# Identity matmuls into an unused bank at idle steps of the mLSTM and GLA mixers

## What is computed

```python
ha = head_rms(mlstm)  * sigmoid(ao)     # A: mLSTM, chunkwise matrix memory with a running maximum
hb = head_rms(gla)    * silu(bg)        # B: gated linear attention, chunkwise
hc = window_fn(rope(cq), rope(ck), cv)  # C: dilated sliding windows over a cache of 2048 rows
hd = sb_fn(dq, dk, dv, b_sb)            # D: stick-breaking attention over paged keys and values
mixed = concatenate([ha, hb, hc, hd]) @ w_out
```

## Time and profile before

| | us |
|---|---|
| median of 3 runs | 2581.53 (2580.14 to 2583.04) |
| the profiled execution, its own time | 2581.21 |
| its span, first to last instruction | 2579.6 |
| TensorE busy in the span | 2360.4 |
| mixers, first layer | 525 to 914 |
| mixers, second layer | 1795 to 2181 |

### The profile page before, as it was taken

How to read it: one execution, slowest core, us unless ns; L and a number is a source line. 1 busy time by engine, 2 the same in 40 slices (tenths; PEclk the granted TensorE clock), 3 DMA queues, 4 the chain that set the end, 5 groups by cost and what they waited for, 6 DMA issues and landing times. The chain is left out here.

```text
span 2579.6 us, 44886 instructions
## 1 busy us (share of the span) xinstructions
PE 2360.4 (92%) x17622; PEld 2094.7 (81%) x17622; DVE 1217.7 (47%) x2088; ACT 933.5 (36%) x1645; POOL 141.3 (5%) x193
## 2 busy tenths in 40 slices
PE   7999999979787889999999999999897877999997
PEld 7999998756545589999999999977564555999997
DVE  6343362253665556332453425522447555653325
ACT  5222342223324455223352334222333255542233
POOL 0000010011221000000000000000112110000000
PEclk8999999989897899999999999999898888999998
DMA  5232343154664343323333333421556535423233
GB/s 136 66 98 82 84 124 121 33 173 147 198 166 138 118 147 83 98 69 94 99 84 82 81 86 111 130 83 55 185 169 185 177 99 168 115 66 98 65 104 97
DMA packets 384957, 290.97 MB, mean 113 GB/s; under 512 B 51808, under 2 KB 368392, under 8 KB 384272
## 3 DMA queue, kind: packets, MB, share of 16 engines
q1 hardware_dynamic: 368128, 234.08, 32.2%
q0 software_dynamic: 16128, 54.54, 6.9%
q10 hardware_dynamic: 528, 0.02, 0.0%
HBM read 274.99 MB, written 13.58 MB: 112 GB/s over the span
## 5 line engine op out<-in xcount | busy, mean ns | idle before, releaser
L218 PE MATMUL ps<-h_hi,w_hi 128*128 128x288 f32 x2400 | 717.8, 299 | 25.0 <-PEq L174 17.9
L219 PE MATMUL ps<-h_lo,w_hi 128*128 128x288 f32 x2400 | 710.2, 296 | 0.0
L220 PE MATMUL ps<-h_hi,w_lo 128*128 128x288 f32 x2400 | 710.1, 296 | 0.0
L242 DVE TENSOR_TENSOR w_lo<-w_raw,w_hi 128x2048 fp32r<-128x2048 f32 x145 | 332.4, 2292 | 340.0 <-ACT w_hi L236 339.9
L218 PEld LDWEIGHTS ps<-h_hi,w_hi 128*128 128x128 f32 x2400 | 452.2, 188 | 31.3 <-issue 25.8
L219 PEld LDWEIGHTS ps<-h_lo,w_hi 128*128 128x128 f32 x2400 | 452.3, 188 | 0.9
L220 PEld LDWEIGHTS ps<-h_hi,w_lo 128*128 128x128 f32 x2400 | 452.2, 188 | 0.0
L236 ACT ACTIVATE w_hi<-w_raw 128x2048 fp32r<-128x2048 f32 x145 | 276.8, 1909 | 163.4 <-PE ps L220 159.1
L218 PE MATMUL ps<-f_a_hi,w_hi 128*128 128x288 f32 x1024 | 302.8, 296 | 0.0
L220 PE MATMUL ps<-f_a_hi,w_lo 128*128 128x288 f32 x1024 | 301.6, 295 | 0.0
L219 PE MATMUL ps<-f_a_lo,w_hi 128*128 128x288 f32 x1024 | 301.5, 294 | 0.0
(11 more groups left out here) (347 smaller groups left out, 3204.3 us busy)
## 6 DMA issues: line engine op xcount, KB each, us to landing
w_raw<-in_w_ffn_in SPq DMA_DIRECT2D x132, 512.0 KB, 5.2
w_raw<-in_w_ffn_out SPq DMA_DIRECT2D x80, 512.0 KB, 4.9
sa_vn<-in_cache_sb_v SPq DMA_DIRECT2D x256, 128.0 KB
w_raw<-in_w_in SPq DMA_DIRECT2D x52, 512.0 KB, 4.5
sa_vn<-in_cache_win_v SPq DMA_DIRECT2D x96, 128.0 KB
w_raw<-in_w_out SPq DMA_DIRECT2D x24, 512.0 KB, 6.5
sa_kn_early<-in_cache_win_k POOLq DMA_DIRECT2D x72, 128.0 KB
sa_vn<-in_cache_win_v SPq DMA_DIRECT2D x16, 512.0 KB
```

The lines of the kernel that those rows point to most:

```text
L218: pe.matmul(out, stat_hi, mov_hi, start=start, stop=False, skip_group_check=True)
L219: pe.matmul(out, stat_hi, mov_lo, start=False, stop=False, skip_group_check=True)
L220: return pe.matmul(out, stat_lo, mov_hi, start=False, stop=stop, skip_group_check=True)
L242: dve.tensor_tensor(E["w_lo"][:, slot], E["w_raw"][:, slot], E["w_hi"][:, slot].bitcast(F32), ALU.subtract).then_inc(S["w_lo"], 1)
```

## The change

A new function issues n matmuls of the identity with itself, each of which overwrites the first 128 columns of a bank that nobody reads at that point. It is called in mLSTM with 6 matmuls ahead of each of the ticks 1, 2 and 3 (steps 2 to 4) and at the head of step 5, with 4 at the end of step 35 and with 6 in each of steps 36, 37 and 38; in GLA with 6 in each of steps 4 and 5. That makes 58 in a layer. The wait for the copied queries moves from step 6 of GLA to the head of step 4.

```diff
--- before.py
+++ after.py
@@ -1337,6 +1337,12 @@
                        "n_turned n_copied")
 
 
+def keep_busy(pe, E, bank, n):
+
+    for _ in range(n):
+        pe.matmul(E["ps"][:, bank, 0:P], E["ident"][:], E["ident"][:], start=True, stop=True, skip_group_check=True)
+
+
 def mlstm(nc, E, M, l, I, O, C, side):
 
 
@@ -1602,9 +1608,10 @@
 
     def tensor_program(pe):
         yield
-        yield
-        yield
-        yield
+        for _ in range(3):
+            keep_busy(pe, E, SC, 6)
+            yield
+        keep_busy(pe, E, SC, 6)
         pe.wait_ge(S["exps_done"], 3)
         n = TILES * H
         for k, row in enumerate((wrow, ws, em)):
@@ -1692,8 +1699,11 @@
         pe.wait_ge(S["s_state_added"], 2 * H)
         pe.transpose(ps[:H, NB, 0:HD], pc[:, :, HD], E["ident"][:HD, :HD])
         pe.transpose(ps[:4 * H, NB, P:2 * P], c0[:, :, :, HD].rearrange("p q h -> p (q h)"), E["ident"][:]).then_inc(S["n_turned"], 1)
-        yield
-        yield from head_tensor(pe, E, S, hA, 2)
+        keep_busy(pe, E, SC, 4)
+        yield
+        for step in head_tensor(pe, E, S, hA, 2):
+            keep_busy(pe, E, SC, 6)
+            yield
 
     return dict(sync=sync_program, tensor=tensor_program, scalar=scalar_program, vector=vector_program)
 
@@ -1916,10 +1926,11 @@
         mm.then_inc(S["pre_done"], 1)
         yield
         yield
-        yield
-        yield
+        pe.wait_ge(M["mx"]["ro_q_out"], TILES)
+        for _ in range(2):
+            keep_busy(pe, E, ATT, 6)
+            yield
         pe.wait_ge(S["factors_ready"], 4)
-        pe.wait_ge(M["mx"]["ro_q_out"], TILES)
         pe.wait_ge(M["mx"]["ro_k_out"], TILES)
 
         def inside(t):
```

## The result

| | us |
|---|---|
| before, median of 5 runs beside it | 2581.42 (2579.19 to 2583.04) |
| after, median of 5 runs | 2593.22 (2590.86 to 2594.15) |
| ratio after to before | 1.0046, 95% interval 1.0031 to 1.0061 |
| the profiled execution of after, its own time and span | 2592.61 and 2591.0 |

The account below looks back on a forecast made before the run. In the mixers TensorE waits, mostly for copies by ScalarE and VectorE. First layer -1.0 + 0.9 - 0.9 = -1.0 us, second +0.3 + 1.1 - 0.9 = +0.5, together -0.5: 2581.0 us, range of all 2575 to 2590.

Parts of the forecast that it names:

- the last one of the sum: Later steps of the stage: ticks 1 to 2 us late find keys and values loaded ahead; counted as nothing.
- GLA: Steps 4 and 5 up to tick 32: 12 matmuls hidden, clock stays up, scores come sooner; -0.9 us in each layer.
- The heads: mLSTM's heads, 22 matmuls: +0.9 us in the first layer, +1.1 us in the second.
- the 2.05 us for step 38's six: mLSTM's heads, behind L1322 towards L1915: nothing hides these six, clock rises in their midst; 2.05 us, first layer.
- The pause of 6.1 us: mLSTM's heads, TensorE's wait for ScalarE's copy: cut to 3 us by steps 36 and 37, half clock still behind it.
- The start: Start of the mixers, 24 matmuls: -1.0 us in the first layer, +0.3 us in the second.
- The sign that I named for it: Start of the mixers, trace after: L1489 about 1 us earlier against the start of the stage, first layer.
- The gain of 1.0 us: L1622 to L1489, first layer: with the clock up these take 1.0 us less and VectorE goes on sooner.
- The first six: Start of the mixers, ahead of tick 1's transposes: 1.3 us, passed through to VectorE's chain.
- the fourth six: Start of the mixers, behind tick 4's transposes, which should find full clock: cost 1.3 us.
- The slower rival: Added matmuls paid at half clock ahead of L1622 and L1915, GLA giving nothing back: +11.2 us, 2593; chance 0.20.
- The faster rival: Clock stays up past the heads too: -4.9 us, about 2576, or 2573 with shorter later half-clock stretches; chance 0.20.

Follow-up runs that it names:

- gla_only: The kernel before with only GLA's 12 matmuls a layer (steps 4 and 5) and the moved wait: 2584.98 us, ratio 1.0026.
- start_only: The kernel before with only the 24 matmuls a layer at the start of mLSTM: 2581.27 us, ratio 1.0005.
- stair_ten: The kernel before with ten identity matmuls a layer in the prompt's attention (851 us), at full clock: 2590.93 us, ratio 1.0068.
- fill_alone: The kernel before with eight identity matmuls a layer in the 2.31 us pause of the prompt's attention, leaving bank 7's sum alone: 2579.61 us, ratio 0.9995.
- stair_four: The kernel before with four identity matmuls a layer in the prompt's attention (851 us), at full clock: 2581.12 us against 2573.44, ratio 1.0031.
- one_column: The whole change, all 116 matmuls and the moved wait, but each matmul multiplies one column in place of 128: 2598.85 us, ratio 1.0080.

## Why the prediction was wrong

**The step that failed** is the last one of the sum: "a tick that comes 1 to 2 us later has its keys and values loaded several units ahead; I count nothing for them". That was argued for transfers, and all that stands behind tick 32 was put at nothing. But how long the clock is at half in those later steps changed. The distance from tick 32 to the mark went from some 166.9 us (three of the four readings of before; 168.4 in the other) to 173.0 us in both layers: 6.1 us twice. Against the second trace of before it is 6.3 us in the first layer, in three places: 2.1 us over GLA's last updates (with step 38's six), 1.9 us some 100 us behind tick 32 and 2.3 us at the end of the prompt's attention (both with GLA's matmuls alone too).

The 12.2 us of this do not add up with the rest to the 11.8 us measured. Against the second trace of before the changed kernel's trace loses 12.3 us behind tick 32 and 5.7 us ahead of it, but that execution of before was the fastest of its ten (2575.4 us). Against the first trace it is 10.7 us behind and 1.9 us ahead, with 1.2 us gained elsewhere. So two thirds or more of the loss are behind tick 32; a finer split is not known.

**What stood ahead of it was right for GLA and too low for the rest.** GLA: forecast -0.9 us in each layer up to tick 32, measured -0.9 and -1.0 from L1925 to there in after, -0.7 and -0.8 in gla_only; tick 32 took 1.06 us for 1.09 forecast, and the clock stayed up. The heads: forecast +0.9 and +1.1, measured +2.0 and +2.3 from L1693 to L1915. The term that was mis-sized is the 2.05 us for step 38's six: they took 2.93 us, at half clock in both layers, in each trace that has them with 128 columns. The pause of 6.1 us was cut to 3.15 as forecast. The start: forecast -1.0 and +0.3; start_only's ratio of 1.0005 does not tell that from nothing. The sign that I named for it failed: L1489 was to come 1.0 us earlier in the first layer, counted from L1451, and came at 32.31 us against 30.36 and 28.66 in the two traces of before. The gain of 1.0 us was read from one trace in which L1622 happened to be at half clock. The first six took 2.93 us in the first layer of after and 1.60 us in its second layer and in start_only, where I had 1.3, and the fourth six 2.39 in the first layer.

**The rivals.** The slower rival had the right sign and nearly the right time (2593, itself past the 2590 at which I ended the range). Its mechanism was payment ahead of L1622 and L1915 at half clock, with GLA's 12 matmuls free. One part of it is borne out: step 38's six ran at half clock to their end and cost some 2 us a layer where they stand, for its 3.1. The rest is not: start_only costs nothing measurable, and GLA's part costs 6.7 us. So the near hit in the number is luck. The faster rival's condition, full clock from L1322 on, did not occur: after was at half from 685.3 to 695.3. It said that shorter half-clock stretches later in the stage might give 3 us more; they do move, but the other way.

**Shown and argued.** Shown: most of the loss sits in steps behind the added matmuls, at stretches of half clock; an unrelated delay of 1.0 us gives 3.3 us a layer there; with the clock kept up over one pause GLA's part, the delay and the heads are level with before, and the whole loses 0.26% of its 0.46%; step 38's six are the rest. Argued: that the added matmuls act through the time at which TensorE reaches the later pauses. The delay shows that this can happen, not that it is how GLA's part acts. Not settled: the rule by which the stretch comes out at 10.2, 13.7 or 17 us (stair_ten had 17 us with the fall inside the pause); why GLA's part, which brings TensorE 1 us earlier and not later, has the long one in every trace without the fill; why the stretch at 820 us comes with GLA's matmuls; why the heads alone with the fill are level with before although they pay for step 38's six; and why the clock falls again at 884.8 us in fill_alone, where part of its 3 us is given back.

## What to carry to other kernels

A change of a microsecond on an engine whose granted clock falls and rises has to be followed to the end of the stage, through every later pause and the stretch at half clock near it (here 10.2 us long in one trace and 13.7 us in another); the sum over the touched steps alone can have the wrong size and sign (here -0.5 us forecast, +11.8 us measured). To find where such a loss sits, add a fixed delay ahead of the suspect or fill the pause that has half clock in it or behind it (here 2.31 us; filled, the clock was 1.00 from 869.0 to 884.8 us), and see whether the loss goes with it. Take a second trace of the kernel before ahead of explaining any stretch, and ahead of the forecast: here one of four stretches differed by 3.5 us and one distance of 190 us by 4.1 us with nothing changed.

## What the runs showed of the hardware that was not expected

- A matmul of one column takes almost the time of one of 128 (12 records: 2.72 against 2.93 us at half clock), yet with it the clock was at half for 20.3 us in a row, from 530.9, with TensorE busy 88% of them. The longest wait of TensorE in that stretch is 1.20 us.
- The wait of 2.31 us for ScalarE had half clock in it (second trace of before, from 869.4 us) or behind it (stair_four, from 874.0 us), and with it filled the clock was 1.00 from 869.0 to 884.8 us (fill_alone). Why the clock of one_column stayed at half through its first stretch, with no wait over 1.20 us, was not shown.
- 1.0 us of work at full clock cost 3.3 us in each layer (stair_four), and eight matmuls placed in a pause 20 us behind it took that back.
- Executions of one kernel spread over 0.4% on this single core: before lay between 2575.5 and 2586.3 us in 31 runs of one batch. In two traces of before the first layer took 193.40 and 189.32 us from L1451 to tick 32. Differences of single traces below 4 us in a layer mean nothing until a second one repeats them.
